# Two on-chip tiles of a two-block transformer kernel begin 32 and 64 bytes behind a multiple of 512 bytes

## The chip, the cores and the metric

The program runs on one core of a Trainium2 chip. The metric is the device time of one execution in microseconds (us), the median of several. TensorE (PE) multiplies matrices: for each product it loads a block of weights (PEld in the profile) and streams a moving operand past it; both come from the on-chip memory SBUF, and the product goes to PSUM. VectorE (DVE), ScalarE (ACT) and GpSimd (POOL) work elementwise on 128 partitions, and DMA queues bring the weights from HBM. An address in SBUF is here the byte within a partition; a tile begins at the same byte in all 128.

## The reference

All data are float32, 512 tokens of width 1024. Two blocks of two layers each follow one another. In the first, each layer is a gated feed-forward half step, a mixer, and another one:

```python
def swiglu(x, w_gate, w_up, w_down):
    return (jax.nn.silu(x @ w_gate) * (x @ w_up)) @ w_down
...
    x = x + 0.5 * swiglu(rmsnorm(x, ffn1_norm), ffn1_gate, ffn1_up, ffn1_down)
    z = rmsnorm(x, mix_norm) @ w_in
...
    y = jnp.concatenate([y_a, y_b.astype(x.dtype), y_c.astype(x.dtype), y_d], axis=-1) @ w_out
    x = x + y
    x = x + 0.5 * swiglu(rmsnorm(x, ffn2_norm), ffn2_gate, ffn2_up, ffn2_down)
```

The mixer of a layer has four parts of width 256: attention with a selection of keys, gated linear attention, a causal convolution over 31 taps, and attention with low-rank queries and keys. The second block has one layer with dilated attention beside a state space model and one with a gated linear recurrence, each followed by a feed-forward step of the same form. All six feed-forward steps have a hidden width of 2816.

## The kernel before

**Split products.** Nearly all large products are made in a fast float32 form (fp32r in the trace) from two parts of each operand: a rounded one ("hi") and what it leaves over ("lo"). One block of 128 x 128 weights gives three matmuls into the same bank: hi weights times hi input, lo weights times hi input, hi weights times lo input. In the plain form that is `split_product` (lines 967, 968 and 969), with moving operands of 512 columns. From the second feed-forward step on, gate and up products go through a scheme that replaces eight block products by seven (`pe_ffn7`, lines 1077, 1079 and 1080), with 256 columns each. Smaller products are made in plain float32 in a single matmul.

**Where the operands lie.** The tile `wring` (16 KB per partition, a ring of four slots of 128 x 1024 numbers) receives every weight from HBM. ACT rounds a slot into `w_hi`, which lies over the tile `scratch` (line 1704, or 1716 by halves). DVE then writes the rest over the slot itself: `w_lo` lies over `wring` (line 2341). In the seven-product scheme DVE and POOL first form sums of weight blocks in `p_raw` (lines 2369, 2371, 2375, 3252), and DVE writes the rests into `p_lo_tile` (line 2355); both lie over the tile `att_diag`. The tile `att_diag` also holds `xn_hi`, the hi part of a normalised input or of a mixer's output (with `xn_more`, which follows it). The inputs `xn`, `xn_lo` and `t_hi_early` lie over `xn`, and `h_hi`, `h_lo`, `g_hi`, `g_lo`, `f_hi`, `f_lo`, `t_lo`, `t_hi_late`, `z_hi` over `arena`.

**How tiles are placed.** Tiles follow one another in SBUF. `sb` begins one at the next multiple of 32 bytes; `sb_aligned` puts a gap ahead of it so that it begins at a multiple of 512 bytes. Seven tiles are placed so: `x`, `xn`, `wring`, `scratch`, `bias`, `arena`, `att_diag`. All slots and blocks within them that the split products read begin at multiples of 512 bytes too. Behind `att_diag` come without gaps `xn_more`, `hpad` (the padded input of the convolution, 2168 bytes for each of two channel blocks), `cst` (the constants), rows and columns of gains, and `small`. By the sizes, `cst` begins 256 bytes behind a multiple of 512, the constant `swap` in it (its column 3545) at 100 bytes behind one, and tap j of the convolution reads `hpad` from 4*j bytes on.

**Order.** Every engine has a queue written out by hand, with semaphores between them. In a feed-forward step a slot of `wring` is loaded again when PE is through with it (gate, up and down in the plain form, down in both) or when its block rests are written (gate and up in the seven-product form); ACT waits for the DMA, DVE for ACT, PE for DVE.

Of the kernel before, what the change touches and what calls it, by code (L numbers as in the profile page):

```python
# [16 lines left out]
P = 128  # L17
SEQ = 512
TB = SEQ // P
D = 1024  # L20
KD = D // P
# [9 lines left out]
B_HEADS, B_KEY, B_VAL, B_CHUNK, B_RANK = 4, 32, 64, 64, 16  # L31
# [318 lines left out]
def program(nc, I, out):  # L350
    ctx = ExitStack()
    with ctx:
        at = {}

        def sb(name, shape, dt=F32):
            at[name] = -(-nc.sbuf_base // 32) * 32
            return ctx.enter_context(nc.sbuf_tensor(name, shape, dt))
# [8 lines left out]

        ALIGN = 512

        def sb_aligned(name, shape):
            gap = -(-(-nc.sbuf_base // 32) * 32) % ALIGN  # L370
            if gap:
                ctx.enter_context(nc.sbuf_tensor(f"gap_before_{name}", [P, gap // 4], F32))
            return sb(name, shape)

        x = sb_aligned("x", [P, KD, SEQ])
        xn = sb_aligned("xn", [P, KD, SEQ])
        y = xn
        wring = sb_aligned("wring", [P, 2, KD, 256])
        scratch = sb_aligned("scratch", [P, 11, SEQ])
        bias = sb_aligned("bias", [P, A_HEADS, SEQ])  # L380
        arena = sb_aligned("arena", [P, 46, SEQ])
        att_diag = sb_aligned("att_diag", [P, TB, B_HEADS, P])
        xn_more = sb("xn_more", [P, 2, SEQ])
        hpad = sb("hpad", [P, 2, TAPS - 1 + SEQ])
        b_mn, b_la = xn_more[:, 0, :], xn_more[:, 1, :]
# [3014 lines left out]
```

## Time and profile before

| what | value |
|---|---|
| device time, median of 3 runs | 3348.34 us (3347.93 to 3349.71) |
| device time of the profiled execution | 3347.23 us |
| its span, first to last instruction | 3345.3 us |
| PE busy | 3225.4 us (96%), 17624 matmuls |
| weight loads (PEld) busy | 2674.3 us (80%) |
| DVE busy | 2158.3 us (65%) |
| ACT busy | 1476.1 us (44%) |
| POOL busy | 449.1 us (13%) |
| mean granted TensorE clock | 0.989 of 2.4 GHz |

Busy shares are those of the profiled execution. A matmul's busy time contains what it overlaps with its neighbours, so the time that one costs in a row of matmuls is read from start to start, not from its own length. The time outside the span is 3347.23 - 3345.3 = 1.9 us.

### The profile page before, as it was taken

The page shows a single profiled execution, that of the slowest core. Times are in us where ns is not written, and L with a number is a line of the kernel's source. Part 1 is how long each engine was busy: PE and PEld are TensorE (multiplying, and loading weights), DVE is VectorE, ACT ScalarE, POOL GpSimd, SP SyncE. Part 2 cuts the span into 40 slices and gives each one's busy share as a digit, 9 for nine tenths or more (in the row PEclk, how much of TensorE's full clock was granted, in tenths as well). Part 3 has the DMA queues.
Part 4 walks back from the last instruction along what each step waited for, and adds up shares of the span by engine and source line. Part 5 has one row for each costly group of instructions (what it writes and reads, how often), then busy time and mean ns, then how long its engine had stood idle before and what let it go on. Part 6 is the DMA issues. An engine that isn't in the chain of part 4 may idle for free.

```text
span 3345.3 us, 49759 instructions
## 1 busy us (share of the span) xinstructions
PE 3225.4 (96%) x17624; PEld 2674.3 (80%) x17624; DVE 2158.3 (65%) x3335; ACT 1476.1 (44%) x2617; POOL 449.1 (13%) x285
## 2 busy tenths in 40 slices
PE   7999999899999999999899999999899999999998
PEld 5888775679988899876578998566689986779986
DVE  3332398748854886388938873844388736678853
ACT  4332345535543554245535653213355534555543
POOL 1110002111100111000202110401021103112100
PEclk9999999999999999999999999999999999999999
DMA  4333231023333333232013332341123323223332
GB/s 137 100 94 97 85 89 58 1 82 95 105 98 98 89 102 104 95 82 84 1 51 89 105 103 94 95 93 38 51 82 107 100 95 95 74 78 101 100 99 78
DMA packets 420149, 286.35 MB, mean 86 GB/s; under 512 B 57416, under 2 KB 395180, under 8 KB 419884
## 3 DMA queue, kind: packets, MB, share of 16 engines
q1 hardware_dynamic: 419200, 283.62, 28.6%
q8 instruction: 74, 1.21, 0.1%
q10 hardware_dynamic: 828, 1.13, 0.1%
q14 instruction: 47, 0.39, 0.0%
HBM read 280.24 MB, written 4.47 MB: 85 GB/s over the span
## 4 chain that ended last, share of the span: by engine, by line
PE 84%; DVE 6%; issue 5%; ACT 2%; POOL 2%; DMA 0%; ACTq 0%; DVEq 0%; SPq 0%; POOLq 0%
PE bank L967 15%; PE bank L969 14%; PE bank L968 14%; PE bank L1077 9%; PE bank L1079 9%; PE bank L1080 9%; PE bank L1457 3%; POOL arena L3246 1%; PE bank L962 1%; PE bank L1337 1%; PE bank L1336 1%; PE bank L1355 1%; PE bank L1451 1%; PE bank L1577 1%; DVE small L2605 1%
## 5 line engine op out<-in xcount | busy, mean ns | idle before, releaser
L2341 DVE TENSOR_TENSOR w_lo<-wring,w_hi 128x1024 fp32r<-128x1024 f32 x298 | 375.7, 1263 | 623.6 <-ACT w_hi L1704 623.4
L1080 PE MATMUL bank<-t_lo,w_hi 128*128 128x256 f32 x2520 | 713.7, 283 | 0.0
L1704 ACT ACTIVATE w_hi<-wring 128x1024 fp32r<-128x1024 f32 x310 | 326.7, 1059 | 735.1 <-DMA wring<-in_ffn_down 295.0
L1080 PEld LDWEIGHTS bank<-t_lo,w_hi 128*128 128x128 f32 x2520 | 484.3, 192 | 0.0
L1077 PE MATMUL bank<-t_hi_early,w_hi 128*128 128x256 f32 x1440 | 408.4, 284 | 9.0 <-ACT scratch L1793 5.4
L1079 PE MATMUL bank<-t_hi_early,p_lo_tile 128*128 128x256 f32 x1440 | 407.6, 283 | 0.0
L969 PE MATMUL bank<-xn_lo,w_hi 128*128 128x512 f32 (+1 forms) x1032 | 403.3, 391 | 0.0
L967 PE MATMUL bank<-g_hi,w_hi 128*128 (+1 forms) x880 | 342.4, 389 | 0.0
L968 PE MATMUL bank<-g_hi,w_lo 128*128 (+1 forms) x880 | 342.4, 389 | 0.0
L969 PE MATMUL bank<-g_lo,w_hi 128*128 (+1 forms) x880 | 342.3, 389 | 0.0
L1077 PE MATMUL bank<-t_hi_late,w_hi 128*128 128x256 f32 x1080 | 307.0, 284 | 13.8 <-ACT scratch L1793 11.7
L2355 DVE TENSOR_TENSOR p_lo_tile<-p_raw,w_hi 128x512 fp32r<-128x512 f32 x360 | 282.5, 805 | 52.4 <-ACT w_hi L1716 52.4
L1079 PE MATMUL bank<-t_hi_late,p_lo_tile 128*128 128x256 f32 x1080 | 306.2, 283 | 0.0
L967 PE MATMUL bank<-xn_hi,w_hi 128*128 128x512 f32 x728 | 287.2, 395 | 8.4 <-DVE xn_lo L2330 7.0
L1077 PEld LDWEIGHTS bank<-t_hi_early,w_hi 128*128 128x128 f32 x1440 | 276.5, 192 | 11.0 <-issue 6.2
L968 PE MATMUL bank<-xn_hi,w_lo 128*128 128x512 f32 x728 | 283.9, 390 | 0.0
L1079 PEld LDWEIGHTS bank<-t_hi_early,p_lo_tile 128*128 128x128 f32 x1440 | 276.5, 192 | 0.2
L1716 ACT ACTIVATE w_hi<-p_raw 128x512 fp32r<-128x512 f32 x360 | 222.5, 630 | 118.0 <-POOL p_raw L3252 58.1
L1793 ACT ACTIVATE scratch<-bank 128x256 f32<-128x256 f32 x360 | 137.9, 383 | 278.8 <-PE bank L1080 263.6
L3252 POOL TENSOR_TENSOR p_raw<-wring 128x512 f32<-128x512 f32 x90 | 133.2, 1481 | 710.9 <-PE bank L1080 710.9
L969 PEld LDWEIGHTS bank<-xn_lo,w_hi 128*128 128x128 f32 (+1 forms) x1032 | 194.3, 188 | 41.5
L3227 POOL TENSOR_TENSOR arena<-arena 128x512 f32<-128x512 f32 x49 | 74.1, 1529 | 1138.1 <-ACT arena L2171 434.4
(451 smaller groups left out, 6420.9 us busy)
## 6 DMA issues: line engine op xcount, KB each, us to landing
wring<-in_ffn_gate SPq DMA_DIRECT2D x88, 512.0 KB, 3.7
wring<-in_ffn_up SPq DMA_DIRECT2D x88, 512.0 KB, 3.8
wring<-in_ffn_down SPq DMA_DIRECT2D x88, 512.0 KB, 3.4
wring<-in_ffn_w_gate SPq DMA_DIRECT2D x44, 512.0 KB, 3.7
wring<-in_ffn_w_up SPq DMA_DIRECT2D x44, 512.0 KB, 3.8
wring<-in_ffn_w_down SPq DMA_DIRECT2D x44, 512.0 KB, 3.3
wring<-in_w_in SPq DMA_DIRECT2D x34, 512.0 KB, 3.6
wring<-in_w_out SPq DMA_DIRECT2D x16, 512.0 KB, 3.3
```

Of the source, the lines that this page charges most:

```text
L967: nc.tensor.matmul(ps, w_hi[:, slot, t, 0:M], hi, start=start, stop=False)
L968: nc.tensor.matmul(ps, w_lo[:, slot, t, 0:M], hi, start=False, stop=False)
L969: return nc.tensor.matmul(ps, w_hi[:, slot, t, 0:M], lo, start=False, stop=stop)
L1077: nc.tensor.matmul(ps, hi[:, k, :], t_hi(j)[:, k, :], start=(not again and k == 0), stop=False, skip_group_check=again)
L1079: nc.tensor.matmul(ps, lo[:, k, :], t_hi(j)[:, k, :], start=False, stop=False, skip_group_check=again)
L1080: mm = nc.tensor.matmul(ps, hi[:, k, :], t_lo[:, j, k, :], start=False, stop=(k == KH - 1), skip_group_check=again)
L1704: nc.scalar.activation(w_hi[:, slot, :, :].rearrange("p k c -> p (k c)"), wunit[:, slot, :], ACT.Copy).then_inc(u_hi.h, 1)
L1716: nc.scalar.activation(p_hi_tile(st, j).rearrange("p k c -> p (k c)"), src, ACT.Copy).then_inc(u_hi.h, 1)
L1793: nc.scalar.activation(dst, src, ACT.Copy).then_inc(p_copied.h, 1)
L2341: nc.vector.tensor_tensor(w_lo[:, slot, :, :].rearrange("p k c -> p (k c)"), wunit[:, slot, :], w_hi[:, slot, :, :].rearrange("p k c -> p ...
L2355: tt(p_lo_tile[:, j, :], src, p_hi_tile(st, j).rearrange("p k c -> p (k c)").bitcast(F32), ALU.subtract).then_inc(u_lo.h, 1)
L3252: tt(p_raw[:, 4, :], raw(st, kind, 0, 0), raw(st, kind, 1, 0), ALU.subtract).then_inc(sg_scaled.h, 1)
```

## The change

`sb_aligned` takes a third argument, the number of bytes behind a multiple of 512 at which the tile is to begin. Two of the seven tiles use it: `wring` (with `w_lo` over it) begins 32 bytes behind, and `att_diag` (with `xn_hi`, `p_raw` and `p_lo_tile` over it) begins 64 bytes behind.

```diff
-        def sb_aligned(name, shape):
-            gap = -(-(-nc.sbuf_base // 32) * 32) % ALIGN
+        def sb_aligned(name, shape, past=0):
+            gap = (past - (-(-nc.sbuf_base // 32) * 32)) % ALIGN
             if gap:
                 ctx.enter_context(nc.sbuf_tensor(f"gap_before_{name}", [P, gap // 4], F32))
             return sb(name, shape)
...
-        wring = sb_aligned("wring", [P, 2, KD, 256])
+        wring = sb_aligned("wring", [P, 2, KD, 256], 32)
         scratch = sb_aligned("scratch", [P, 11, SEQ])
         bias = sb_aligned("bias", [P, A_HEADS, SEQ])
         arena = sb_aligned("arena", [P, 46, SEQ])
-        att_diag = sb_aligned("att_diag", [P, TB, B_HEADS, P])
+        att_diag = sb_aligned("att_diag", [P, TB, B_HEADS, P], 64)
```

`scratch`, `bias` and `arena` stay at multiples of 512 bytes, each 512 bytes further on than before, since a gap of 480 bytes now stands behind `wring`. The tiles behind `att_diag` have no gaps of their own and move along: their distance from a multiple of 512 grows by 64 bytes (`cst` from 256 to 320, `swap` from 100 to 164). No instruction is added, removed or moved on any engine: PE, DVE, ACT, POOL and the DMA queues have the same instructions in the same order, with other addresses in them.

## Rows read from the trace of the kernel before

**Rows 1.** The page: busy time, queue q1, the chain by engine.
```profile
PE 3225.4 (96%) x17624; PEld 2674.3 (80%) x17624; DVE 2158.3 (65%) x3335; ACT 1476.1 (44%) x2617; POOL 449.1 (13%) x285
...
q1 hardware_dynamic: 419200, 283.62, 28.6%
...
PE 84%; DVE 6%; issue 5%; ACT 2%; POOL 2%; DMA 0%; ACTq 0%; DVEq 0%; SPq 0%; POOLq 0%
```
**Rows 2.** Timeline of PE: start us, length us, instruction; two matmuls stand between.
```profile
2909.21 0.39 PE L967 MATMUL bank<-xn_hi,w_hi 128*128 128x512 f32 x1
...
2909.89 0.39 PE L967 MATMUL bank<-xn_hi,w_hi 128*128 128x512 f32 x1
```
**Rows 3.** Timeline of PE, seven-product scheme; two matmuls stand between.
```profile
830.00 0.28 PE L1079 MATMUL bank<-t_hi_late,p_lo_tile 128*128 128x256 f32 x1
...
830.36 0.28 PE L1079 MATMUL bank<-t_hi_late,p_lo_tile 128*128 128x256 f32 x1
```
**Rows 4.** Groups by line and shape: matmuls with an operand that moves.
```profile
L1079 PE MATMUL bank<-t_hi_early,p_lo_tile 128*128 128x256 f32 x1440 | 407.6, 283 | 0.0
L1079 PE MATMUL bank<-t_hi_late,p_lo_tile 128*128 128x256 f32 x1080 | 306.2, 283 | 0.0
L967 PE MATMUL bank<-xn_hi,w_hi 128*128 128x512 f32 x728 | 287.2, 395 | 8.4 <-DVE xn_lo L2330 7.0 <-POOL w_lo L3273 1.1 <-DVE w_lo L2341 0.3
L968 PEld LDWEIGHTS bank<-g_hi,w_lo 128*128 128x128 f32 x880 | 165.2, 188 | 34.0
L968 PE MATMUL bank<-xn_hi,w_lo 128*128 128x512 f32 x728 | 283.9, 390 | 0.0
L968 PE MATMUL bank<-f_hi,w_lo 128*128 128x512 f32 x320 | 126.2, 394 | 0.0
L968 PE MATMUL bank<-z_hi,w_lo 128*128 128x512 f32 x288 | 113.2, 393 | 0.0
L968 PEld LDWEIGHTS bank<-h_hi,w_lo 128*128 128x128 f32 x176 | 33.0, 188 | 6.9
L1187 PE MATMUL bank<-w_lo,z_hi 128*128 128x512 f32 x64 | 24.9, 390 | 0.0
```
**Rows 5.** By line: plain float32 matmuls; duration ns min/median/max (L1500 reads `swap`).
```profile
L1500 PE MATMUL bank<-arena,cst x8: 592/592/648, 2182.1 to 2210.2; 128*128 128x512 f32 x8
L1457 PE MATMUL bank<-xn,wring x192: 592/592/1201, 2112.3 to 2229.3; 128*128 128x512 f32 x192
```
**Rows 6.** By line, DVE: duration ns min/median/max, first and last start.
```profile
L2625 DVE SCALAR_TENSOR_TENSOR arena<-hpad,cur_dw,arena x120: 742/752/1879, 421.7 to 1522.1; 128x512 f32<-128x512 f32 x120
L2330 DVE SCALAR_TENSOR_TENSOR f_lo<-x,col,f_hi x40: 737/742/752, 716.1 to 2977.8; 128x512 fp32r<-128x512 f32 x40
L2341 DVE TENSOR_TENSOR w_lo<-wring,w_hi x298: 1206/1225/2311, 29.0 to 3307.2; 128x1024 fp32r<-128x1024 f32 x149
```
**Rows 7.** Windows: length, busy PE, PEld, DVE, ACT, POOL, clock, DMA share, GB/s.
```profile
780.00:940.00 160.00, 160.00 (x1335) 160.00 (x1335) 140.35 (x233) 94.23 (x200) 22.36 (x16) 1.00 0.36 106
960.00:1060.00 100.00, 100.00 (x443) 82.81 (x442) 32.88 (x36) 28.51 (x37) 0.00 (x0) 1.00 0.30 99
```
**Rows 8.** Groups of DVE from 780 to 940 us that read or write moved tiles.
```profile
L2355 DVE TENSOR_TENSOR p_lo_tile<-p_raw,w_hi 128x512 fp32r<-128x512 f32 x65 | 51.9, 818 | 9.1 <-ACT w_hi L1716 9.1
L2355 DVE TENSOR_TENSOR p_lo_tile<-wring,w_hi 128x512 fp32r<-128x512 f32 x48 | 32.8, 684 | 10.0 <-ACT w_hi L1716 10.0
...
L2371 DVE TENSOR_TENSOR p_raw<-p_raw,wring 128x512 f32<-128x512 f32 x16 | 11.1, 694 | 0.6
```
**Rows 9.** DMA issues: tile and source, count, KB each, median us to landing.
```profile
wring<-in_ffn_gate SPq DMA_DIRECT2D x88, 512.0 KB, 3.7
...
wring<-in_ffn_down SPq DMA_DIRECT2D x88, 512.0 KB, 3.4
```
**Rows 10.** Waits: engine, line, what ended it: us in total, times, longest us.
```profile
ACT w_hi L1704 <- DMA wring<-in_ffn_down: 295.0, 76, 4.5
...
PE bank L1591 <- DMA relb<-in_rel_bias: 9.8, 1, 9.8
...
PE bank L1598 <- DMA arena<-in_x: 2.4, 1, 2.4
```

## The prediction

> **What bounds the kernel now.** I read the page first, then the windows of two long stretches, then PE's timeline within them. The page puts 84% of the chain that ended last on PE and 0% on DMA; PE is busy for 3225.4 of 3345.3 us [rows 1]. The windows show the same without an average: from 780 to 940 us (seven-product scheme) and from 960 to 1060 us (down products) PE is busy for all 160.00 and all 100.00 us, at full clock, while DVE has 140.35 of 160 and 32.88 of 100 us of work, and the DMA engines 0.36 and 0.30 [rows 7]. So time is gained or lost where one matmul of a row takes longer or shorter, nearly nowhere else. What one costs is read from start to start: three matmuls of 512 columns take 2909.89 - 2909.21 = 0.68 us, 226.7 ns each [rows 2], three of 256 columns 830.36 - 830.00 = 0.36 us, 120 ns each [rows 3]. The difference is 106.7 ns for 256 columns, 0.417 ns a column, one column in a cycle of 2.4 GHz; what is left is 120 - 106.7 = 13.3 ns, the same at both lengths. That is a fixed cost of each split matmul, and both operands of all of them begin at multiples of 512 bytes.
>
> **The change part by part.** It changes addresses only; no instruction, wait or queue is different. Each kind of access to a moved tile is a term.
>
> *TensorE, count.* Lo weights out of `wring`, 32 bytes behind: 880 + 728 + 320 + 288 + 176 = 2392 at line 968, and 64 at line 1187, where they are the moving operand. Lo weights out of `att_diag`, 64 bytes behind: 1440 + 1080 = 2520 at line 1079. `xn_hi` as the moving operand, 64 bytes behind: 728 at line 967, and the 728 of line 968 that are counted already [rows 4]. Together 2392 + 64 + 2520 + 728 = 5704 matmuls with one operand or two off the multiple of 512. One cycle more or less on each would be 5704 x 0.417 ns = 2.4 us.
>
> *TensorE, price.* The trace has no split matmul with an operand off a multiple of 512, so the price is bounded from both sides by the nearest rows. Nearest are the plain float32 matmuls of line 1500: their weights are the constant `swap`, 100 bytes behind a multiple of 512, further off and less even than anything the change makes, and they take 592 ns; those of line 1457, both operands on multiples of 512, of the same 512 columns, take 592 ns too [rows 5]. That is a difference of nothing. Two things keep this from being proof: a plain matmul of 512 columns lasts 592 ns against 390 for a split one [rows 2, 5], 0.2 us more or about one more cycle a column, so a read has more room in it, and `swap` stands on the side of the weights, not of the moving operand. Upper bound: an operand that begins between two pieces of memory costs one more piece; at 32 bytes that is 8 numbers, 8 x 0.417 = 3.3 ns, at 64 bytes 16 numbers, 6.7 ns. With 2392 + 64 - 728 = 1728 matmuls at 32 bytes alone and 2520 + 728 + 728 = 3976 with a 64-byte operand this is 5.8 + 26.5 = 32 us. Lower bound: the whole fixed part of 13.3 ns disappears from them, 5704 x 13.3 ns = 76 us less. I take 0, by line 1500, and keep both ends.
>
> *VectorE.* The best scale is the convolution: tap j reads `hpad` at 4*j bytes, so hardly any of its 120 instructions starts on a multiple of 32. They take 752 ns in the median and 742 at least; line 2330, the same operation with all operands on multiples of 512, 742 [rows 6]. So an offset costs 0 to 10 ns. In the seven-product stretch 65 + 48 + 3 x 16 = 161 instructions touch moved tiles (`p_raw` has two further groups of 16 of the same length) [rows 8]: at most 1.6 us, where DVE has 160 - 140.35 = 19.65 us free [rows 7]. Over the program, even 10 ns on all of its 3335 instructions would be 33 us, against 3345.3 - 2158.3 = 1187 us without DVE work [rows 1]. What hides it is PE's own work, which runs on through it; if that cover were gone, these 33 us would be the most that it costs. On the path: 0.
>
> *ScalarE and GpSimd.* They read the ring and `p_raw` too. ACT has 44% and POOL 13% of the span [rows 1], and ACT in the two windows 94.23 and 28.51 us [rows 7]. The same 10 ns on all 2617 instructions of ACT would be 26 us, beside PE as well. On the path: 0.
>
> *DMA.* Each load writes into the ring, now at 32 bytes behind. The mean packet of q1 takes 0.286 x 16 x 3345.3 us / 419200 = 36.5 ns [rows 1]. How little packets matter is shown by two loads of 512 KB: `ffn_down` arrives in rows of 4096 bytes after 3.4 us, `ffn_gate` in rows of 512 bytes, eight times as many, after 3.7 us [rows 9]. If an offset cut packets once more, 0.3 us a load is a generous bound. It falls into slack: in the down stretch ACT is already waiting for the DMA, 295.0 us in 76 waits [rows 10], and PE still does not pause [rows 7], because three other slots of 24 x 0.227 = 5.4 us each lie ahead of the slot that is being filled: 16.3 us of cover for 3.4 us of load, 1.2 us for the rests [rows 6] and about as much for the rounding ahead of them. PE waits for a DMA only at the very start, 9.8 and 2.4 us, for `relb` and for `x`, and neither lands in the ring [rows 10]. On the path: 0.
>
> The Trainium skill speaks against the change here. "DMA: Bandwidth & Descriptors", section How a descriptor splits into AXI transactions, says that transactions start at multiples of 256 bytes, so that a descriptor that begins off one is cut once more. By its figures a 512-byte row at 32 bytes behind would be 17 beats in three transactions in place of 16 in two, an estimate of 6% on the packet's data. Taken onto the packet above that would be some 2 ns, and the sum would stay as it is, since the cover is the same; no row of this trace has a packet of the ring off such a multiple.
>
> *Sum.* 0 on every term: a profiled execution of 3347.2 us as before (3345.3 of span and 1.9 around it). The median of the runs lies 1.1 us above the profiled one, so the forecast is the median itself, 3348.3 us.
>
> **The rivals.**
>
> *Slower: the moving stream or the lo weights pay for their offset.* Place: lines 968, 1079 and 967 with `xn_hi`, all on PE's path, where nothing hides a nanosecond. Price: one piece more on each, 8 columns' time as the middle case, 5704 x 3.3 = 19 us, so 3367; 32 us at the upper bound, 3380. It decides from 6.7 us (0.2%) on, which is 1.2 ns or three cycles per matmul. For it: the split form reads a number per cycle and operand, twice the rate of the plain one, and is untested off 512. Against it: `swap` [rows 5] and the convolution [rows 6], which do without any such cost.
>
> *Faster: the fixed 13.3 ns is two reads in each other's way.* The weights of the next matmul are loaded while the moving operand streams, and before the change both begin in the same phase. If that is what the 13.3 ns are, another phase frees them on matmuls whose operands now differ: 76 us, 3272. For it: the cost is equal at both lengths [rows 2, 3], as a clash per load would be. Against it: a load of 128 numbers and a stream of 256 or 512 would meet at other moments for different lengths, while the remainder is the same to a nanosecond; it looks like a fixed step of the form. The Trainium skill, "TensorE: Matmul & The Clock Gate", section Back-to-back issue gap, gives N/2.4 + 2.5 ns for one matmul after another; by that a 512-column one would take 215.8 ns, and 11 of the 13.3 ns would be something else than a floor. This trace does not agree with the figure, and shows 226.7 ns [rows 2].
>
> *VectorE becomes the bound of the seven-product stretches.* 19.65 us free over 161 instructions is 122 ns each [rows 7, 8]; below that PE feels nothing. The convolution shows 10 ns at most. Even at 250 ns each it would be (250 - 122) x 161 = 21 us in this window of 160 us, and six times that at least in the program, so 3470. Hardly likely.
>
> *Nothing is moved.* Were gaps absorbed elsewhere, the time would be the same: it is in the forecast.
>
> **How the numbers follow.** A measurement of this kernel can tell 0.2%, 6.7 us, from no change. Forecast, no effect: 0.61. PE slower by its operands: 0.21, and DVE the bound: 0.01, together slower 0.22. PE faster by another phase: 0.17, of which a third is a gain of less than 20 us, on some of the pairs only. The predicted time is 3348.3. The range goes from 3330 to 3382: it takes the forecast, the slower case to its upper bound, and the small gains, about 0.85 in all; the full gain of 76 us stays outside. Faster 0.17, same 0.61, slower 0.22.
>
> **What would show it.** In the profile after, starts within a row of split matmuls stay 226.7 and 120 ns apart on lines 967, 968 and 1079; PE stays busy for all of both windows; lines 2341 and 2355 keep their median to within 10 ns; the ring's loads keep landing after 3.3 to 3.8 us. If the starts behind a matmul of line 968 or 1079 move and those of line 1077 or 969 do not, the TensorE term was wrong, and its size is read straight from there. If the starts stay and the span grows, the windows of PE will show gaps, and what ended them names the term.

## The result and the profile after

The kernel with the change takes 3373.99 us in the median of four runs (3373.52 to 3375.17), the kernel before 3349.03 beside it (3347.93 to 3354.53): a ratio of 1.0071, 95% interval 1.0056 to 1.0086. That is 25 us more where no change was forecast. The page after, with busy time, q1 and the chain, answers to [rows 1]:

```profile
PE 3254.7 (97%) x17624; PEld 2661.5 (79%) x17624; DVE 2158.4 (64%) x3335; ACT 1477.5 (44%) x2617; POOL 459.4 (14%) x285
...
q1 hardware_dynamic: 419200, 283.62, 29.3%
...
PE 87%; DVE 5%; issue 4%; ACT 2%; POOL 2%; DMA 0%; ACTq 0%; DVEq 0%; SPq 0%; POOLq 0%
```

The span grew by 26.5 us (3345.3 to 3371.8), PE's busy time by 29.3, and its share of the chain went from 84 to 87%. DVE and ACT stayed within 1.4 us; POOL's busy time rose by 10.3 us, which is taken up below. The two windows of [rows 7], columns as there:

```profile
780.00:940.00 160.00, 155.98 (x1300) 154.96 (x1299) 141.16 (x229) 92.81 (x195) 28.12 (x16) 0.99 0.37 102
960.00:1060.00 100.00, 100.00 (x456) 81.58 (x455) 37.58 (x46) 32.55 (x45) 0.00 (x0) 1.00 0.29 95
```

The 4 us without PE in the first are no new wait. The program is already 16 us late there, so the opening of the scheme's stage (its first matmul starts at 781.5 us after, 765.7 before) now falls into the window. In both kernels PE waits 3.4 us for ACT in that opening, the last time until 795 us after and 780 before. In the second window PE never pauses. So the time is in the matmuls themselves, and only their starts show it. Timeline of PE after, down products (start us, length us):

```profile
990.39 0.40 PE L967 MATMUL bank<-g_hi,w_hi 128*128 x1
990.62 0.39 PE L968 MATMUL bank<-g_hi,w_lo 128*128 x1
990.85 0.40 PE L969 MATMUL bank<-g_lo,w_hi 128*128 x1
991.09 0.40 PE L967 MATMUL bank<-g_hi,w_hi 128*128 x1
...
992.49 0.40 PE L967 MATMUL bank<-g_hi,w_hi 128*128 x1
```

Nine matmuls take 992.49 - 990.39 = 2.10 us, 233.3 ns each in place of 226.7 [rows 2], 700 in place of 680 a triple. The seven-product scheme went the other way:

```profile
849.78 0.28 PE L1079 MATMUL bank<-t_hi_early,p_lo_tile 128*128 128x256 f32 x1
...
851.19 0.28 PE L1079 MATMUL bank<-t_hi_early,p_lo_tile 128*128 128x256 f32 x1
```

Twelve matmuls (eleven stand between) take 1.41 us, 117.5 ns each in place of 120 [rows 3]. Summed over the program, each start on PE to the next start:

| from a start to PE's next start, us in total | before | after | difference |
|---|---|---|---|
| lines 967 to 969 (7248 matmuls, 512 columns) | 1663.9 | 1709.0 | +45.1 |
| lines 1077 to 1080 (7560 matmuls, 256 columns) | 935.9 | 918.3 | -17.6 |
| everything else on PE, pauses included | 731.8 | 731.0 | -0.8 |
| together | 3331.5 | 3358.3 | +26.8 |

These 26.8 us are the 26.5 of the span. The first row is also met by counting: 880 + 176 + 320 + 288 = 1664 triples at 20 ns more are 33.3 us, the 728 with `xn_hi` at 16 ns 12.

### The profile page after: what moved, and what is told of

Read it like the earlier page. It is cut to its first block, busy times and chain, and to the rows that moved or that the text cites. A ratio compares the mean times of both kernels' runs of the same rounds, so it can differ in the third digit from the quotient of the medians.

```text
span 3371.8 us, 49759 instructions
## 1 busy us (share of the span) xinstructions
PE 3254.7 (97%) x17624; PEld 2661.5 (79%) x17624; DVE 2158.4 (64%) x3335; ACT 1477.5 (44%) x2617; POOL 459.4 (14%) x285
## 3 DMA queue, kind: packets, MB, share of 16 engines
q1 hardware_dynamic: 419200, 283.62, 29.3%
## 4 chain that ended last, share of the span: by engine, by line
PE 87%; DVE 5%; issue 4%; ACT 2%; POOL 2%; DMA 0%; ACTq 0%; DVEq 0%; SPq 0%; POOLq 0%
PE bank L967 16%; PE bank L969 15%; PE bank L968 15%; PE bank L1079 8%; PE bank L1077 8%; PE bank L1080 8%; PE bank L1457 3%; POOL arena L3246 1%; PE bank L962 1%; PE bank L1337 1%; PE bank L1336 1%; PE bank L1355 1%; PE bank L1451 1%; PE bank L1577 1%; DVE small L2781 1%
## 5 line engine op out<-in xcount | busy, mean ns | idle before, releaser
L1080 PEld LDWEIGHTS bank<-t_lo,w_hi 128*128 128x128 f32 x2520 | 474.6, 188 | 0.0
L967 PE MATMUL bank<-g_hi,w_hi 128*128 (+1 forms) x880 | 351.9, 400 | 0.0
L1077 PE MATMUL bank<-t_hi_late,w_hi 128*128 128x256 f32 x1080 | 305.1, 283 | 14.1 <-ACT scratch L1793 11.7
L3252 POOL TENSOR_TENSOR p_raw<-wring 128x512 f32<-128x512 f32 x90 | 141.8, 1576 | 687.2 <-PE bank L1080 687.2
```

What stands on the lines that cost most here:

```text
L967: nc.tensor.matmul(ps, w_hi[:, slot, t, 0:M], hi, start=start, stop=False)
L1077: nc.tensor.matmul(ps, hi[:, k, :], t_hi(j)[:, k, :], start=(not again and k == 0), stop=False, skip_group_check=again)
L1080: mm = nc.tensor.matmul(ps, hi[:, k, :], t_lo[:, j, k, :], start=False, stop=(k == KH - 1), skip_group_check=again)
L3252: tt(p_raw[:, 4, :], raw(st, kind, 0, 0), raw(st, kind, 1, 0), ALU.subtract).then_inc(sg_scaled.h, 1)
```

## The experiments

The table gives the places of the operands in bytes behind a multiple of 512. "512, ns" is the mean time of a triple (the three matmuls of lines 967 to 969) with moving operands out of `arena`, "xn, ns" that of triples with `xn_hi`, both good to about 1 ns. "256, ns" is the median interval in the scheme, or two where its stages differ. "512 us" and "256 us" are the sums of the table above, less those of before. The device times of e9 and e10 are medians of four executions, that of e12 of six; each other experiment ran once. The rest of the program ("everything else") differs from kernel to kernel by up to 9 us (730 to 739), so the single executions are read by their intervals, of which each has thousands.

| kernel | w_hi, w_lo | arena, xn_hi | p_lo | 512, ns | xn, ns | 256, ns | 512 us | 256 us | device us (before beside it) |
|---|---|---|---|---|---|---|---|---|---|
| before | 0, 0 | 0, 0 | 0 | 680 | 680 | 120 | | | |
| after | 0, 32 | 0, 64 | 64 | 700 | 697 | 118 | +45.1 | -17.6 | 3373.99 (3349.03) |
| e1_ring32 | 0, 32 | 0, 0 | 0 | 700 | 700 | 120 | +47.7 | +2.9 | 3400.85 (3347.2) |
| e2_diag64 | 0, 0 | 0, 64 | 64 | 680 | 696 | 118 | +13.3 | -12.8 | 3349.8 (3347.2) |
| e3_all32 | 32, 32 | 32, 32 | 32 | 680 | 680 | 120 | +0.5 | +1.5 | 3353.5 (3347.2) |
| e4_weights32 | 32, 32 | 0, 0 | 0 | 700 | 700 | 118 | +46.5 | -17.5 | 3374.62 (3347.2) |
| e5_hi32 | 32, 0 | 0, 0 | 0 | 696 | 696 | 118 | +34.8 | -12.2 | 3376.47 (3349.61) |
| e6_moving32 | 0, 0 | 32, 0 | 0 | 700 | 680 | 117 | +30.8 | -23.3 | 3355.36 (3349.61) |
| e7_weights64_diag64 | 64, 64 | 0, 64 | 64 | 700 | 687 | 113 and 118 | +36.9 | -25.3 | 3358.13 (3349.61) |
| e8_weights256 | 256, 256 | 0, 0 | 0 | 680 | 680 | 120 | +0.5 | +1.5 | 3352.59 (3349.61) |
| e9_rests64 | 0, 0 | 0, 0 | 64 | 680 | 680 | 118 | +1.8 | -14.3 | 3334.28 (3349.87) |
| e10_products64 | 0, 0 (p_hi 64) | 0, 0 | 64 | 680 | 680 | 113 and 118 | -0.4 | -31.7 | 3314.88 (3349.87) |
| e11_weights128 | 128, 128 | 0, 0 | 128 | 698 | 699 | 119 | +41.2 | -10.6 | 3381.46 (3349.87) |
| e12_products192 | 0, 0 (p_hi 192) | 0, 0 | 192 | 680 | 680 | 118 | +2.7 | -14.1 | 3342.11 (3348.73) |

**The theories.** A: what counts is the distance between the weights and the moving operand that PE reads at the same time; absolute addresses do not matter. Two readings of it differ in which weights are meant: A-own takes the block with which a matmul computes, A-next the block that is being loaded meanwhile for the next one. B: an operand off a multiple of 512 is dear by itself. C: the cost comes from something else that the change does along the way, such as `scratch`, `bias` and `arena` sitting 512 bytes further on.

**One part at a time: e1 and e2.**

```diff
-        wring = sb_aligned("wring", [P, 2, KD, 256])
+        wring = sb_aligned("wring", [P, 2, KD, 256], 32)
```

> Only the ring (w_lo) begins 32 bytes behind, att_diag is back at a multiple of 512. What starts to start shows in the changed kernel: 239, 228 and 233 ns on lines 967, 968, 969 with g_hi (before 227, 227, 227), 118 ns in the seven-product scheme (before 120). Theory A (what counts is how the weights that are loaded during a matmul lie against its moving operand): lines 967 to 969 with g_hi, f_hi, h_hi, z_hi stay at 239, 228, 233 and those with xn_hi join them; the seven-product scheme, whose lo weights lie in att_diag, goes back to 120. That keeps the loss of some 45 us and gives up the gain of some 17: about 3395 us. Theory B (an operand off a multiple of 512 bytes is dear by itself, whichever other is read): only line 968, and at most the line ahead of it, are slower, the seven-product scheme as fast as before: about 3360 us. Theory C (the cause is a side effect, such as the 512 bytes by which arena and scratch moved): as the changed kernel, 3374 us.

```diff
-        att_diag = sb_aligned("att_diag", [P, TB, B_HEADS, P])
+        att_diag = sb_aligned("att_diag", [P, TB, B_HEADS, P], 64)
```

> Only att_diag (p_lo_tile, xn_hi) begins 64 bytes behind, the ring is back at a multiple of 512. Theory A: 227 ns in the down products, 118 in the seven-product scheme, a few ns more on matmuls with xn_hi as moving operand (728 triples): 3348 - 17 + 3 to 6, about 3335 us, faster than both kernels. Theory B: line 1079 slower than 120 ns, above 3348 us. Theory C: 3348 us, since scratch and arena lie as before.

The parts separate. The ring alone makes every triple of 512 columns dear and leaves the scheme, which takes nothing out of the ring on PE, at 120 ns; `att_diag` alone makes only the `xn_hi` triples dear (696 ns in place of 680, where those out of `arena` stay at 680) and the scheme cheaper. e2 was expected at 3335 us under A and took 3349.8: the price of the `xn_hi` triples had been put at 3 to 6 us and was 13.3, and the scheme gave 12.8 in place of 17. Theory A held in e2 by the intervals, not by the time. Timeline of PE in e1:

```profile
1000.13 0.40 PE L967 MATMUL bank<-g_hi,w_hi 128*128 x1
1000.37 0.39 PE L968 MATMUL bank<-g_hi,w_lo 128*128 x1
1000.60 0.40 PE L969 MATMUL bank<-g_lo,w_hi 128*128 x1
1000.83 0.40 PE L967 MATMUL bank<-g_hi,w_hi 128*128 x1
...
1002.93 0.40 PE L967 MATMUL bank<-g_hi,w_hi 128*128 x1
```

Twelve take 2.80 us, 233.3 each. Within the triple the intervals are in the mean 239, 228 and 233 ns: the dearest is line 967, whose own operands both still begin at multiples of 512, and the one with `w_lo` is the cheapest. While it streams, the load for line 968 is running, as PE's loads after show:

```profile
990.39 0.19 PEld L968 LDWEIGHTS bank<-g_hi,w_lo 128*128 128x128 f32 x1
990.63 0.19 PEld L969 LDWEIGHTS bank<-g_lo,w_hi 128*128 128x128 f32 x1
```

The load of `w_lo` starts with the matmul of line 967 (990.39) and takes 0.19 us. This speaks for A-next. The device time of e1 lies 54 us above before, of which 51 are the two groups and 3 the rest; 3395 us were expected and 3400.85 measured.

**All tiles together: e3.**

```diff
-        x = sb_aligned("x", [P, KD, SEQ])
-        xn = sb_aligned("xn", [P, KD, SEQ])
+        x = sb_aligned("x", [P, KD, SEQ], 32)
+        xn = sb_aligned("xn", [P, KD, SEQ], 32)
...
-        arena = sb_aligned("arena", [P, 46, SEQ])
-        att_diag = sb_aligned("att_diag", [P, TB, B_HEADS, P])
+        arena = sb_aligned("arena", [P, 46, SEQ], 32)
+        att_diag = sb_aligned("att_diag", [P, TB, B_HEADS, P], 32)
```

(`wring`, `scratch` and `bias` likewise, 32 each.)

> All seven tiles begin 32 bytes behind a multiple of 512, so that every operand is off it but the distances between operands are those of before. Theory A: as before, 227 and 120 ns, 3348 us. Theory B: every split matmul is slower, by what line 968 lost or more: above 3390 us. Theory C: no statement, since everything moves.

Not one split operand begins at a multiple of 512 here, and each interval is as before:

```profile
990.24 0.39 PE L967 MATMUL bank<-g_hi,w_hi 128*128 x1
...
990.92 0.39 PE L967 MATMUL bank<-g_hi,w_hi 128*128 x1
```

Three in 0.68 us, as in [rows 2]. That ends B, and B was the slower rival of the prediction.

**The weights without the inputs, and the inputs without the weights: e4, e5, e6.**

```diff
-        wring = sb_aligned("wring", [P, 2, KD, 256])
-        scratch = sb_aligned("scratch", [P, 11, SEQ])
+        wring = sb_aligned("wring", [P, 2, KD, 256], 32)
+        scratch = sb_aligned("scratch", [P, 11, SEQ], 32)
```

> Ring and scratch both begin 32 bytes behind: hi and lo weights of lines 967 to 969 lie alike to each other, the moving operands 32 bytes away. In the seven-product scheme hi weights are 32 bytes behind, lo weights and moving operands at a multiple. Theory A: whatever the distance of 32 bytes costs now falls on every matmul of a triple alike: one and the same value for lines 967, 968, 969, not 239, 228, 233; if it is the distance from the moving operand alone, 239 each, some 30 us more than the ring alone: about 3430 us. If instead it is the distance between one block of weights and the next (theory A2), 227 each in lines 967 to 969: about 3348 us. Theory B: about as A, each line slower.

e5 is the line of `scratch` of e4 alone, so that only `w_hi` moves:

> Only scratch (w_hi) begins 32 bytes behind; lo weights and moving operands are at multiples of 512. The weights for the next matmul begin to load 3 to 4 ns after a matmul starts, so two readings of theory A are left. A-next (the block that is being loaded counts): with the ring alone off, line 967, during which w_lo was loaded, took 239 ns; now the offset blocks are loaded during lines 968 and 969, so line 968 or 969 is the slowest and line 967 below them. A-own (the block that is in use counts): lines 967 and 969, which use w_hi, are slow and line 968 near 227. In both the triple costs about 700 ns as it did with the ring alone and with both (before 680), and the seven-product scheme goes to 118 as with both: about 3375 us.

```diff
-        arena = sb_aligned("arena", [P, 46, SEQ])
+        arena = sb_aligned("arena", [P, 46, SEQ], 32)
```

> Only arena begins 32 bytes behind, with all moving operands of 512 columns but xn_hi and xn_lo; the weights are at multiples of 512, so the distance is the same 32 bytes with the other sign. Theory A with a cost that depends on the size alone: 234 ns on lines 967 to 969 with f, g, h and z, 226.7 with xn, 118 in the seven-product scheme with t_lo: about 3365 us. Theory A with a cost that depends on the sign: another value, perhaps below 227 ns. Theory B (offsets are dear by themselves): has fallen with all seven tiles at 32 bytes, and would say 234 as well.

In e6 the weights stand to one another as before and only the moving operands out of `arena` move. PE's timeline, five matmuls between:

```profile
1000.24 0.39 PE L967 MATMUL bank<-g_hi,w_hi 128*128 x1
...
1001.64 0.39 PE L967 MATMUL bank<-g_hi,w_hi 128*128 x1
```

Six in 1.40 us, 233.3 each, while the triples with `xn_hi`, whose two operands did not move, stay at 680 in the same execution. So it is the distance between the weights and the moving operand, and not between one block of weights and the next. e4 confirms it from the other side: both weights moved, inputs not, 700 again. Its expected time of 3430 us (each matmul at 239 ns) was missed, though: all three lines have 233 ns, and the kernel took 3374.62. e6 was expected at 3365 and took 3355.36, mainly since its scheme ran at 117 ns and not at 118.

What these three do not give is the choice between A-own and A-next. If each mismatched matmul paid by itself, e4 with three mismatches in a triple should cost more than e1 with one; both are 700. In e5 A-own would have line 968 cheapest, whose `w_lo` stands at 0 like `g_hi`, and A-next line 967, during which that `w_lo` is loaded. The means are 230.8, 233.1 and 231.7 ns on lines 967, 968 and 969. Line 967 is the cheapest and line 968 the dearest, as A-next has it, but the means are 2 ns apart where most single intervals lie between 229 and 240. The price is one of the whole triple; that the load sets it is likely by e1 and e5 and not settled.

**Other distances: e7, e8, e11.** e7 puts `wring`, `scratch` and `att_diag` at 64, e8 `wring` and `scratch` at 256, e11 `wring`, `scratch` and the views `p_lo_tile` and `p_raw` at 128. Of e7:

```diff
-        wring = sb_aligned("wring", [P, 2, KD, 256])
-        scratch = sb_aligned("scratch", [P, 11, SEQ])
+        wring = sb_aligned("wring", [P, 2, KD, 256], 64)
+        scratch = sb_aligned("scratch", [P, 11, SEQ], 64)
...
-        att_diag = sb_aligned("att_diag", [P, TB, B_HEADS, P])
+        att_diag = sb_aligned("att_diag", [P, TB, B_HEADS, P], 64)
```

> Hi and lo weights and att_diag all begin 64 bytes behind, xn and arena at multiples. Theory A: xn_hi lies to w_hi as before, at distance 0, xn_lo 64 bytes from it, g and f 64 bytes from both weights. So lines 967 with xn_hi back near 227 to 230 ns, those with g and f all alike at the value for 64 bytes, between 227 and 234 if the cost falls with distance, above 234 if it grows. Seven-product scheme 118 ns if any distance helps it. If only the pattern within 32 bytes matters, as a clash of pieces of memory would, 64 bytes are as good as 0: 227 everywhere, 120 in the scheme, 3348 us.

> Hi and lo weights begin 256 bytes behind, att_diag at a multiple of 512, so hi weights and p_lo_tile are 256 bytes apart. If the cost repeats with 256 bytes or a part of it (banks of memory in turn): 227 and 120 ns, 3348 us. If it depends on the distance up to 512 bytes: another value; 64-byte steps that grew dearer would give 240 ns and more, and half the 512 bytes would be the best place if the cost comes from two reads that meet: below 227.

> Hi and lo weights and p_lo_tile begin 128 bytes behind, moving operands (xn_hi too) at multiples of 512. At 32 and 64 bytes a triple of 512-column matmuls took 700 ns, at 0 and 256 bytes 680. If the cost repeats with 128 bytes: 680 ns and 120 in the scheme, 3348 us. If it repeats with 256 bytes only: 700 ns or more, and below 120 in the scheme: 3350 to 3380 us.

At 256 everything is as before, five matmuls between in 1.36 us for six:

```profile
999.68 0.39 PE L967 MATMUL bank<-g_hi,w_hi 128*128 x1
...
1001.04 0.39 PE L967 MATMUL bank<-g_hi,w_hi 128*128 x1
```

So a distance of 256 bytes counts as none, and since `bias` and `arena` sit 512 bytes further on here too, without effect, C falls (e9, below, moves no tile at all and still changes the scheme). Between 32, 64 and 128 the price of a 512-column triple hardly differs: 700, 700, 698. (The single execution of e11 took 3381.46 us, just outside the 3350 to 3380 that were expected of it.) In e7 the `xn_hi` triples have a distance on line 969 alone (`xn_lo` stayed at 0) and take 687: one mismatched pair can also cost 7 ns in place of 20. The scheme does differ, and not in order of distance: 118 at 32, 119 at 128, and in e7 113.3 ns in its first stage:

```profile
849.80 0.28 PE L1077 MATMUL bank<-t_hi_early,w_hi 128*128 128x256 f32 x1
...
850.48 0.28 PE L1077 MATMUL bank<-t_hi_early,w_hi 128*128 128x256 f32 x1
```

Six in 0.68 us. The other four stages of the same execution have a median of 118, with the same operands at the same addresses.

**Taking the gain and leaving the loss: e9, e10, e12.** If a distance between weights and moving operand slows 512 columns and speeds 256, only the scheme's weights should have one.

```diff
-        p_lo_tile = over("p_lo_tile", [P, 8, BLK], "att_diag")
-        p_raw = nc.alloc_sbuf_tensor_at("p_raw", [P, 8, BLK], F32, offset=at["att_diag"])
+        p_lo_tile = over("p_lo_tile", [P, 8, BLK], "att_diag", 64)
+        p_raw = nc.alloc_sbuf_tensor_at("p_raw", [P, 8, BLK], F32, offset=at["att_diag"] + 64)
```

> Ring, scratch, att_diag, xn and arena all at multiples of 512 as before; only the views p_lo_tile and p_raw over att_diag begin 64 bytes further on. It takes from the change its gain and leaves its cost. Theory A (distance between the operands of neighbouring reads, told apart form by form): the 512-column matmuls stay at 226.7 ns with every operand, xn_hi among them, and the seven-product scheme goes from 120 to 118 ns, 7560 matmuls x 2 ns = 15 us less: about 3333 us. Rival (the gain in the scheme needs the other tiles that moved as well, or is a state of the chip): 3348 us.

e10 adds the hi parts of the sums and products, in a view 64 bytes into `scratch`. It needs more than addresses. There is a hole behind `scratch`'s eighth row. A sum of blocks (`r34`) moves into the tile `rows`. And in a stage's opening ACT waits one matmul group longer before it rounds products 1 and 3, since a shifted block touches its neighbour's last bytes. So e10 against before is not a change of distance alone; e12 is, against e10:

```diff
-        scratch = sb_aligned("scratch", [P, 11, SEQ])
+        scratch = sb_aligned("scratch", [P, 8, SEQ])
+        sb("hole", [P, P])
+        scratch_b = sb("scratch_b", [P, 3, SEQ])
...
+        p_hi_all = over("p_hi_all", [P, SLOTS, KD, P], "scratch", 64)
...
-            return w_hi[:, st.slot(4 + j // 2), KH * (j % 2):KH * (j % 2 + 1), :]
+            return p_hi_all[:, st.slot(4 + j // 2), KH * (j % 2):KH * (j % 2 + 1), :]
...
+            act.e.wait_ge(unit_ps.h, st.units + 5 + 1)
             product_hi(1, 0, 0)
-            act.e.wait_ge(unit_ps.h, st.units + 5 + 1)
             product_hi(2, 0, 0)
+            act.e.wait_ge(unit_ps.h, st.units + 6 + 1)
             product_hi(3, 0, 0)
-            act.e.wait_ge(unit_ps.h, st.units + 6 + 1)
```

> As the one with only p_lo_tile and p_raw shifted, and the hi blocks of the seven-product scheme are shifted by 64 bytes as well (a view of their own over scratch, with 512 bytes of hole behind its first eight tiles, the later three tiles of scratch behind that; the partial sums of r34 lie in the tile of rows, which is free after the start; two roundings at the start of a scheme wait for one unit more). All weights of the scheme are 64 bytes from all its moving operands, while those of 512 columns keep their distances. In the kernel with weights and att_diag at 64 bytes the scheme took 113.3 ns per matmul in one of its stages and 118 in the others. Theory A: the scheme at 118 or below, 226.7 ns elsewhere: 3324 us if it is as there (25 us less), 3298 us if all stages go to 113.3 ns. Rival: the two waits at the start of five stages cost what the distance gains, about 3340 us.

e12 is e10 with 192 in place of 64:

> As the kernel with all weights of the seven-product scheme shifted by 64 bytes, but by 192 bytes. The runs so far leave two readings. If the cost depends on the distance within 256 bytes, whichever operand lies ahead, 192 is as good as 64 (192 = 256 - 64): 113 to 118 ns per matmul in the scheme, 226.7 ns elsewhere, about 3315 us. If what helps is that the weights begin a little behind the moving operand, 192 bytes are another case, and with all operands of the scheme at 128 bytes it took 119: about 3340 us.

Against the kernel before the ratios are 0.9951 (0.9935 to 0.9968) for e9, 0.9889 (0.9872 to 0.9906) for e10 and 0.9972 (0.9959 to 0.9984) for e12. In all three the 512-column triples stay at 680. e10 in a stage with the fast rhythm, eight matmuls between (its lines are numbered three higher):

```profile
1199.95 0.28 PE L1080 MATMUL bank<-t_hi_late,p_hi_all 128*128 128x256 f32 x1
...
1200.97 0.28 PE L1080 MATMUL bank<-t_hi_late,p_hi_all 128*128 128x256 f32 x1
```

and e12 at the same place:

```profile
1199.99 0.28 PE L1080 MATMUL bank<-t_hi_late,p_hi_all 128*128 128x256 f32 x1
...
1201.05 0.28 PE L1080 MATMUL bank<-t_hi_late,p_hi_all 128*128 128x256 f32 x1
```

Nine in 1.02 us are 113.3 ns, nine in 1.06 us 117.8. The medians of e10's five stages are 118, 113, 113, 118 and 113, those of e12 118 throughout. The fast rhythm of 113 ns has been seen only at 64 bytes with hi and lo weights both moved (e7 and e10), never at 192 in e12's five stages. So the expectation that 192 is as good as 64, whichever operand lies ahead (3315 us), failed; the other reading, about 3340 us, is near the 3342.11 measured.

e10's gain is accounted for: 31.7 us in the scheme of its profiled execution, 3314.0 us of span against 3345.3. In the profiled executions of e12 and e9 the scheme gives 14.1 and 14.3 us, but the rest takes 7.3 and 6.0 more. Most of that goes with TensorE's clock. Matched instruction by instruction with before, 5.5 us of it lie between 550 and 650 us of the program in both. Windows from 590 to 612 us, columns as in [rows 7], before and then e12:

```profile
590.00:612.00 22.00, 18.32 (x135) 16.19 (x136) 19.81 (x59) 10.94 (x26) 0.64 (x1) 0.84 0.01 2
590.00:612.00 22.00, 16.63 (x86) 14.76 (x85) 15.49 (x43) 7.73 (x15) 0.00 (x0) 0.61 0.00 0
```

The granted clock is 0.84 of 2.4 GHz there before and 0.61 in e12, and PE starts 86 matmuls in place of 135. e9, e3 and e8 have 0.61 there too and lose the same 5.5 us in that part of the program; e10 and e7 have 0.84 and lose about 1. Why some kernels get the lower clock there is open. e10 is the fastest of all kernels here.

## Why the prediction was wrong

**What bounds the kernel: right.** PE sets the time and nothing else does. All 26.5 us are in PE's intervals.

**TensorE, count: right as a count of matmuls whose own operand moved, but the wrong thing to count.** 5704 matmuls were taken to be touched. In fact all 7248 of lines 967 to 969 are dearer or share a triple with a dearer one, and all 7560 of the scheme are cheaper, those of lines 1077 and 1080 too, whose own operands stand as before.

**TensorE, price: the step that failed.** The prediction put 0 on this term and took it from line 1500, a plain float32 matmul whose weights stand off a multiple of 512. Measured were +45.1 us on the 512-column split matmuls and -17.6 us on those of 256. The row itself holds after as well, with `swap` now 164 bytes behind, and so does line 1457, whose weights come out of the moved ring (by line, lengths in ns min/median/max; then stretches of the timeline, after and before):

```profile
L1457 PE MATMUL bank<-xn,wring x192: 592/592/1201, 2132.4 to 2249.4; 128*128 128x512 f32 x192
...
2139.76 2.74 PE L1457 MATMUL bank<-xn,wring 128*128 128x512 f32 x6
...
2117.49 4.88 PE L1457 MATMUL bank<-xn,wring 128*128 128x512 f32 x11
```

Those 592 ns are a matmul's recorded length, which overlaps its neighbours. From start to start it is (2.74 - 0.592) / 5 = 0.43 us after, with weights 32 bytes off their moving operand, and (4.88 - 0.592) / 10 = 0.43 us before. The prediction compared lengths (592 against 390) where starts were to be compared (429 against 227 ns); the difference of 0.2 us came out the same by luck. The plain form doesn't show the effect at all, and so could say nothing of the split one. The text had named that doubt ("a read has more room in it") and then gone by the row nevertheless. The second mistake was one sign for all: the price is +6.2 ns a matmul at 512 columns and -2.3 at 256, in the mean of all, and a sum of nothing would have needed both to be nothing. The gain of 17.6 lies within the lower bound of 76, the loss of 45.1 beyond the upper one of 32; their sum of 27 hides that, and falls inside the margin only because they cancel in part. That upper bound was built of pieces of 32 and 64 bytes, 3.3 and 6.7 ns. No run shows such a piece: 32, 64 and 128 bytes cost a triple the same 18 to 20 ns.

**The range: luck.** 3374 us lies within 3330 to 3382. The upper part of the range was there for the slower rival, whose mechanism the runs refute, so the range held the time without having its cause.

**The slower rival: the right side and nearly the right size, for a wrong reason.** It gave 3367, and 3374 was measured. But it said that an operand pays for its own offset: e3 has every operand offset and pays nothing, and the dearest matmul after is one with no offset operand. Its middle price of 3.3 ns on 5704 matmuls is near the total only because a larger loss and a gain happen to leave that much.

**The faster rival came nearest to the mechanism.** It said "two reads in each other's way": weights that are loaded beside a moving stream, and the phase between them. The runs show that the distance between the two counts, and make it likely, not certain, that the load is the read that matters. The 13.3 ns are indeed no floor: e10 has 113.3 - 106.7 = 6.7 ns. Its flaw was that another phase need not be a better one. It is so for 256 columns; for 512 it is worse, 20 ns a matmul over the columns' time in place of 13.3. The argument against it, that the remainder of 13.3 ns is equal at both lengths, drew a law from two points at one and the same phase.

The Trainium skill, "SBUF — State Buffer", section Who interferes with whom, gives TensorE two read ports, one for the moving operand and one for the load of weights, and calls them independent. These runs do not agree for the split form: where the two operands stand to one another changes the interval by 2 to 3% (e3 against e4 and e6), though no run shows whether that happens at the ports or behind them.

**VectorE, ScalarE, GpSimd: right that none of them reaches the path.** Line 2341 keeps 1225 ns, the convolution 752 [rows 6]; line 2355 has 684 in the median before and after:

```profile
L2341 DVE TENSOR_TENSOR w_lo<-wring,w_hi x298: 1206/1225/2312, 28.7 to 3333.3; 128x1024 fp32r<-128x1024 f32 x149
L2355 DVE TENSOR_TENSOR p_lo_tile<-p_raw,w_hi x360: 676/684/1789, 782.3 to 3220.7; 128x512 fp32r<-128x512 f32 x180
```

GpSimd's line 3252 (`p_raw` from `wring`) went from 1466 to 1521 ns in the median. It costs nothing: POOL idles 687 us before that line, waiting for PE. Nor is it the tiles' own offset: e1 and e4 have `wring` and `p_raw` at the same places, and line 3252 takes 1467 ns in e1 and 1520 in e4. It is longer in the kernels whose scheme runs faster than 120 ns; why is open.

**DMA: right about the cover, the size a little over its bound.** The bound was 0.3 us a load. `ffn_gate` lost just that against [rows 9], but `ffn_w_gate` and `ffn_w_up` lost 0.4 (3.7 to 4.1 and 3.8 to 4.2), and the sign "after 3.3 to 3.8 us" was missed (tile and source, count, KB, median us to landing):

```profile
wring<-in_ffn_gate SPq DMA_DIRECT2D x88, 512.0 KB, 4.0
...
wring<-in_ffn_down SPq DMA_DIRECT2D x88, 512.0 KB, 3.4
...
wring<-in_ffn_w_up SPq DMA_DIRECT2D x44, 512.0 KB, 4.2
```

The mean packet of q1 went from 36.5 to 0.293 x 16 x 3371.8 us / 419200 = 37.7 ns. It costs PE nothing: PE waits for a DMA only at the start, 9.6 and 2.3 us, as before. In e8, at 256 bytes, `ffn_gate` lands in 3.7 us again:

```profile
wring<-in_ffn_gate SPq DMA_DIRECT2D x88, 512.0 KB, 3.7
```

The rule of the Trainium skill that the prediction weighed, "DMA: Bandwidth & Descriptors", section How a descriptor splits into AXI transactions, agrees with that: rows of 512 bytes land later with the ring off a multiple of 256 and not at one, and `ffn_down` with its rows of 4096 bytes hardly changes (3.4 to 3.5). Its 6%, an estimate, stands beside 8% on the landing and 3% on the mean packet, which mixes both lengths of rows. It agrees in direction alone: in e7 and e11, with the ring at 64 and 128 bytes, `ffn_gate` lands after 4.0 us too, no later than at 32.

## What to carry to other kernels

A row of back-to-back split matmuls has a price that depends on where its weights stand to its moving operand within 256 bytes, and the better distance differs by the number of columns: measure start to start, by form, after every change of the memory layout, also one made for another reason. A row of another form of instruction, however like it looks, is no bound for the price of this one; where the doubtful form has no row, the range should hold its whole margin, per form and with either sign. Where a layout has one tile for two uses, give each use its own view, as e9 and e10 do, rather than one distance for the tile. And when single executions differ by a few us, compare the granted clock in the same stretch before naming a cause.

## What the runs showed of the hardware

- In the split form the interval is 226.7 ns for 512 columns where weights and moving operand begin at the same distance from a multiple of 256 bytes (before, e3, e8). It is about 232 to 233 in the mean of a triple where they do not, at 32, 64 or 128 bytes apart and whichever of the two moved (e1, e4 to e6, e11, and e7 out of `arena`). For 256 columns it is 120 ns against 113.3 to 119.
- The plain float32 form has 429 ns from start to start for 512 columns, whether its weights lie 0 (before), 32 (after) or 128 bytes (e11) off the moving operand (line 1457).
- One load off phase (e1) costs a triple as much as three (e4), another one (`xn_hi` in e7) a third of it, and in e1 within the triple the dearest matmul is the one during which that load runs.
- One kernel has more than one rhythm. In e7 and e10 the scheme runs at 113 ns in some of its five stages and at 118 in the others, at the same addresses. What chooses is open; if all five of e10's stages ran at 113.3, this would be worth (118 - 113.3) x 2 x 1512 = 14 us more, an estimate.
- Why the sign differs between 256 and 512 columns is open as well. At both lengths a load starts 2 to 5 ns after a matmul's start. Its recorded length is 0.19 us, longer than a 256-column interval (0.12) and shorter than a 512-column one (0.23).
- The same stretch of the program (590 to 612 us) had a mean granted clock of 0.84 in before, e7 and e10 and of 0.61 in e3, e8, e9 and e12, and the latter four each lost 5.5 us in the part of the program around it.
